# A hybrid decoder layer: convolution of the second tile back on VectorE, small ScalarE steps ahead of pair scalings, and a longer rotation of row slots

## The reference

```
proj = x @ w_in                      # q, k, v | index q, k, weights | z, xbc, dt
A    = sparse attention: 64 keys per query chosen by an index score, softmax, values
B    = Mamba-2 scan of silu(conv4(xbc)), two chunks of 128, gated RMS norm with silu(z)
h    = LayerNorm(alpha * x + concat(A, B) @ w_out)
for each of 8 heads:                 # PEER, "product keys"
    s1, s2 = halves of (h @ wq) against 128 keys each; top 16 of each
    best 16 of the 256 sums -> 16 expert numbers, gate = softmax(best)
    out += sum_k gelu(h . u[expert_k]) * gate_k * v[expert_k]
result = LayerNorm(alpha * h + out)
```

## Time and profile before

| what | value |
|---|---|
| median of 3 runs | 835.3 us (829.94 to 835.62) |
| profiled execution | 832.65 us, span 830.9 us, mean PE clock 0.83 |
| busy PE / DVE / ACT / POOL | 68% / 65% / 54% / 36% of the span |
| HBM read | 299.5 MB, mean 362 GB/s over the span |
| gathers | 256, 268.45 MB, 78.6% of 16 engines' span |
| first gather issued | 132.4 us |
| chain that ended last | DMA 40%, PE 26%, DVE 19%, ACT 6%, issue 6% |

### The profile page before, as it was taken

The page is one execution under the profiler, slowest core; times in us unless marked ns, Lnnn a source line. Parts: engine busy times, 40 slices in busy tenths (PEclk is TensorE's granted clock), DMA queues, the critical chain, the costliest instruction groups (busy, mean ns, idle before and its releaser), DMA issues.

```text
span 830.9 us, 10111 instructions
## 1 busy us (share of the span) xinstructions
PE 568.8 (68%) x3343; PEld 473.9 (57%) x3343; DVE 542.3 (65%) x1364; ACT 449.3 (54%) x805; POOL 297.9 (36%) x279
## 2 busy tenths in 40 slices
PE   7989999887879888864545555525566565454596
PEld 4458577575569887853544445524455564454542
DVE  3487574485777574848585858469857576767454
ACT  1025137455667665756565657527766566565532
POOL 0000005642444334453535353414754435344400
PEclk9989999899979899967878776767776767867789
DMA  8991005899999999999999999999999999999992
GB/s 300 386 355 52 1 1 204 297 397 354 341 416 411 410 410 410 419 421 422 422 420 422 420 420 420 422 421 382 411 421 421 421 423 422 422 421 423 422 422 109
DMA packets 58521, 301.08 MB, mean 362 GB/s; under 512 B 5576, under 2 KB 16112, under 8 KB 25712
## 3 DMA queue, kind: packets, MB, share of 16 engines
q0 software_dynamic: 36864, 268.45, 78.6%
q1 hardware_dynamic: 20400, 31.92, 10.8%
q10 hardware_dynamic: 1216, 0.19, 0.1%
HBM read 299.49 MB, written 1.05 MB: 362 GB/s over the span
## 4 chain that ended last, share of the span: by engine, by line
DMA 40%; PE 26%; DVE 19%; issue 6%; ACT 6%; POOL 2%; another core or an unknown queue 1%; DVEq 0%; SPq 0%; POOLq 0%; ACTq 0%
DMA arena<-in_expert_uv,expert 34%; PE bank L652 6%; PE bank L502 5%; DMA arena<-in_peer_wq 5%; PE bank L633 5%; DVE arena L1482 5%; PE bank L672 3%; ACT arena L1010 3%; PE bank L514 2%; POOL arena L455 1%; ACT weight L1000 1%; PE bank L617 1%; DVE score L1459 1%; DVE score L1461 1%
## 5 line engine op out<-in xcount | busy, mean ns | idle before, releaser
L455 POOL DMA_INDIRECT arena<-in_expert_uv,expert x256 | 281.4, 1099 | 489.5 <-PE bank L652 260.0
L652 PE MATMUL bank<-ident,arena 128*128 128x128 f32 x1920 | 302.7, 328 | 218.5 <-ACT arena L1010 211.8
L1482 DVE SCALAR_TENSOR_TENSOR arena<-x_sb,arena 128x1024 f32<-128x1024 f32 x256 | 307.9, 1229 | 172.0 <-DMA arena<-in_expert_uv,expert 168.5
L652 PEld LDWEIGHTS bank<-ident,arena 128*128 128x128 f32 x1920 | 279.9, 173 | 241.9 <-ACT arena L1010 233.2
L1010 ACT ACTIVATE arena<-arena,weight 128x1024 f32<-128x1024 f32 x240 | 257.1, 1138 | 2.2
L995 ACT ACTIVATE gelu<-dots 128x4 f32<-128x4 f32 (+2 forms) x76 | 15.5, 204 | 216.7 <-DVE arena L1482 209.1
L502 PE MATMUL bank<-arena,x_t 128*128 128x512 f32 (+1 forms) x128 | 55.1, 585 | 6.1 <-DMA arena<-in_w_idx 6.1
L633 PE MATMUL bank<-x_t,arena 128*128 128x128 f32 x384 | 50.9, 297 | 11.6 <-DMA arena<-in_peer_wq 11.6
L1000 ACT ACTIVATE weight<-gelu,gate 128x1 f32<-128x1 f32 x256 | 55.9, 284 | 3.5
L633 PEld LDWEIGHTS bank<-x_t,arena 128*128 128x128 f32 x384 | 49.7, 213 | 12.2 <-DMA arena<-in_peer_wq 12.2
L502 PEld LDWEIGHTS bank<-arena,x_t 128*128 128x128 f32 x128 | 25.3, 206 | 30.3 <-issue 26.4
(11 more groups left out here) (200 smaller groups left out, 487.6 us busy)
## 6 DMA issues: line engine op xcount, KB each, us to landing
arena<-in_w_in SPq DMA_DIRECT2D x5, 2048.0 KB, 19.8
arena<-in_peer_wq SPq DMA_DIRECT2D x6, 1024.0 KB, 7.4
arena<-in_w_out SPq DMA_DIRECT2D x2, 2048.0 KB, 18.2
arena<-in_expert_uv,expert POOLq DMA_INDIRECT x256
mix<-in_peer_wq SPq DMA_DIRECT2D x2, 1024.0 KB, 16.1
arena<-in_w_idx SPq DMA_DIRECT2D x4, 304.0 KB, 6.7
x_t<-in_x_columns SPq DMA_DIRECT2D x4, 256.0 KB, 5.8
x_sb<-in_w_in SPq DMA_DIRECT2D x1, 1024.0 KB, 9.5
```

Of the source, the lines that this page charges most:

```text
L455: pool.indirect_dma_start(out=arena[:, slot * SLOT:(slot + 1) * SLOT], out_offset=None, in_=expert_uv, in_offset=bass.IndirectOffsetOnAxis ...
L652: last = mm(banks[2 * tile + k // 4][:, (k % 4) * P:(k % 4 + 1) * P], lhsT=arena[:, at + k * P:at + (k + 1) * P], rhs=ident[:, :], is_tran ...
L1482: ins = stt(rows, x_rows[:, bass.ds(tile * D_MODEL, D_MODEL)], 1.0, rows, ALU.mult, ALU.mult, accum_out=dots[:, parity, j:j + 1])
```

## The change

- GpSimd's `convolve_late` and its tables go; VectorE runs `convolve(1, 0)` ahead of the first pair's dots and `convolve(1, 1)` behind them. Slot 1, where `xbc_raw` lies, waits for the convolution.
- `first_slots` has another order; slot 0 takes rows from the 15th gather on. For this, head 1's and 5's weights move into `big` (where q and k lay), loaded when tile 1's logits are done, and the transposed probabilities of tile 1 go into slot 0, over the logits, after all four transposes.
- Key scores of units 1 to 7 alternate between `mid` and `cb_masked`.
- ScalarE: scores, roots and gate exponentials move ahead of neighbouring pair scalings; TensorE's and VectorE's orders follow. `normalise` is split in two (`centre`, `spread`).
- VectorE rotates k's second tile after two of the eight selection rounds of tile 0.

```
-    start = [10, 11, 12, 13, 14, 15, 10, 11, 1, 5, 12, 13, 14, 15, 10, 11]
-    grow = [1, 5, 12, 13, 14, 15, 10, 11, 2, 1, 5, 12, 13, 8, 9, 14]
-    ring = [6, 7, 15, 10, 11, 2, 1, 5, 12, 13, 8, 9, 14]
-    return start + grow + 2 * ring + ring[:6] + ring[6:] + ring[:6] + [0, 4, 3]
+    start = [10, 11, 12, 13, 14, 15, 1, 10, 11, 12, 13, 5, 14, 15, 0, 1]
+    grow = [10, 11, 12, 13, 5, 14, 15, 0, 1, 10, 11, 2, 12, 8, 9, 13]
+    ring = [6, 7, 5, 14, 15, 0, 1, 10, 11, 2, 12, 8, 9, 13]
+    return start + grow + 2 * ring + ring[:4] + ring[4:] + ring[:4] + [4, 3]
...
-        probs_t = [view(mid, 2048, 1, HEADS, P), view(big, 0, TILES, HEADS, P)]
+        probs_t = [view(mid, 2048, 1, HEADS, P), view(arena, SCRATCH, TILES, HEADS, P)]
...
+            if h % 4 == 1:
+                return view(big, 0, KT, 2 * P)
...
-            wait_job(sp, ("T_p", 1, 3))
+            wait_job(sp, ("logits", 1, 3))
             load_head(1)
...
+                        elif slot == 1:
+                            pool.wait_ge(conv_ready, 2 * TILES)
...
-                    if isinstance(u, int) and u == 0 and j in LATE_TAPS:
-                        for n, k in LATE_TAPS[j]:
-                            convolve_late(n, k)
...
             queries(0, 1)
+            scores_of_keys(0, 1)
+            project(("proj_v", 1), "v", 1, ks=range(0, 4))
             sum_group(0, 1)
-            scores_of_keys(0, 1)
-            project(("proj_v", 1), "v", 1)
+            project(("proj_v", 1), "v", 1, ks=range(4, KT))
...
             y_diagonal(1)
+            queries(0, 2)
             sum_group(0, 4)
-            queries(0, 2)
-            sum_group(0, 5)
             scores_of_keys(0, 2)
             project_out(1, 0, ATTN)
-            sum_group(0, 6)
+            sum_group(0, 5)
             project_out(1, 1, ATTN)
             transposed_y(1)
+            sum_group(0, 6)
+            project_out(1, 0, SSD)
             sum_group(0, 7)
-            project_out(1, 0, SSD)
...
             weigh_slots(0, 0, 0)
-            weigh_slots(0, 0, 1)
-            take_queries(0, 1)
-            take_scores(0, 1)
             silu_z(1)
             silu_xbc(1, 0)
             silu_xbc(1, 1)
+            take_queries(0, 1)
+            take_scores(0, 1)
+            weigh_slots(0, 0, 1)
             weigh_slots(0, 0, 2)
             take_v(1)
+            exp_gate(act, 1)
             weigh_slots(0, 0, 3)
-            exp_gate(act, 1)
             take_mixed("T_attn", 0, attn_t_ready, 1)
             weigh_slots(0, 0, 4)
-            weigh_slots(0, 0, 5)
             take_queries(0, 2)
             root_of_squares(1)
+            take_scores(0, 2)
+            weigh_slots(0, 0, 5)
             weigh_slots(0, 0, 6)
-            take_scores(0, 2)
+            take_mixed("T_y", 4, y_t_ready, 1)
+            exp_gate(act, 2)
             weigh_slots(0, 0, 7)
-            take_mixed("T_y", 4, y_t_ready, 1)
             weigh_slots(1, 1, 0)
-            exp_gate(act, 2)
...
-            select_keys(0, range(TOPK_KEYS // 8))
+            select_keys(0, range(0, 2))
             rope_qk(1, 1)
+            select_keys(0, range(2, TOPK_KEYS // 8))
...
+            convolve(1, 0)
             dot_slots(0, 0, 0, 0)
+            convolve(1, 1)
             dot_slots(0, 0, 0, 1)
...
             dot_slots(0, 0, 0, 4)
-            finish_gate(1, 1)
             take_ssd(1)
             dot_slots(0, 0, 0, 5)
             scale_ssd(1)
-            dot_slots(0, 0, 0, 6)
+            finish_gate(1, 1)
             scores_in(0, 2)
             route_sides(2)
+            dot_slots(0, 0, 0, 6)
             dot_slots(0, 0, 0, 7)
```

More of the change, by code:

```diff
@@ L180, in build_layer @@
         attn = view(mid, 3072, HEADS, HEAD_DIM)
-        tap_product = view(arena, at + 1536, 4, P)
-        probs_t = [view(mid, 2048, 1, HEADS, P), view(big, 0, TILES, HEADS, P)]
+        probs_t = [view(mid, 2048, 1, HEADS, P), view(arena, SCRATCH, TILES, HEADS, P)]
         diag = view(mid, 1024, 8, P)
@@ L246, in build_layer @@
         z_ready, raw_ready, conv_ready, silu_ready, v_ready = (sem(n) for n in ("z_ready", "raw_ready", "conv_ready", "silu_ready", "v_ready"))
-        consts_t_ready, late_tap = sem("consts_t_ready"), sem("late_tap")
+        consts_t_ready = sem("consts_t_ready")
         decay_arg_ready, decay_ready, decay_masked = (sem(n) for n in ("decay_arg_ready", "decay_ready", "decay_masked"))
@@ L296, in head_weights @@
         def head_weights(h):
-            if h % 4:
-                return view(arena, (0, 4, 3)[h % 4 - 1] * SLOT, KT, 2 * P)
-            return view(mix, 1024, KT, 2 * P)
+            if h % 4 == 0:
+                return view(mix, 1024, KT, 2 * P)
+            if h % 4 == 1:
+                return view(big, 0, KT, 2 * P)
+            return view(arena, {2: 4, 3: 3}[h % 4] * SLOT, KT, 2 * P)
         def weight_rows(name, k, width=512):
@@ L319, in scores_at @@
         def scores_at(u):
-            if isinstance(u, int) and u < 2:
-                return view(mid, 2560, 2 * N_KEYS)
+            if isinstance(u, int) and u < PEER_HEADS:
+                return cb_masked[:, :, :].rearrange("p a b -> p (a b)") if u and u % 2 == 0 else view(mid, 2560, 2 * N_KEYS)
             return big[:, bass.ds(u * 2 * N_KEYS, 2 * N_KEYS)]
@@ L431, in _ @@
                       allow_small_or_imprecise_dtypes=True).then_inc(consts_ready, 1)
-            last_readers = {0: ("peer_q", 1, 5), 2: ("T_y", 1), 3: ("peer_q", 1, 7), 4: ("peer_q", 1, 6), 5: ("proj_v", 1),
+            last_readers = {0: ("pv", 1), 2: ("T_y", 1), 3: ("peer_q", 1, 7), 4: ("peer_q", 1, 6), 5: ("proj_v", 1),
                             6: ("out", 1, 1), 7: ("out", 1, 1), 8: ("out", 1, 0), 9: ("out", 1, 0), 10: ("proj_xbc", 1, 0),
@@ L448, in gather_unit @@
                             pool.wait_ge(slot_used, len(before) - before[::-1].index(slot))
-                        elif slot in last_readers:
+                        elif slot == 1:
+                            pool.wait_ge(conv_ready, 2 * TILES)
+                        else:
                             wait_job(pool, last_readers[slot])
@@ L926, in take_probs @@
             def take_probs(t):
+                wait_job(act, ("T_p", t, 2 * t + 1))
                 for n in range(2 * (t + 1)):
@@ L1364, in half_stats, with centre @@
                 link(nc.vector.bn_stats(stats[:, 6 * half:6 * half + 6], x_sb[:, t, part]))
-            def normalise(t, n, done):
+            halves = [slice(half * 512, (half + 1) * 512) for half in range(2)]
+            def centre(t):
                 link(nc.vector.bn_aggr(moments[:, :], stats[:, :]))
                 ts(rstd[:, :], moments[:, 1:2], LN_EPS, None, ALU.add).then_inc(var_ready, 1)
-                halves = [slice(half * 512, (half + 1) * 512) for half in range(2)]
                 for part in halves:
@@ L1373, in normalise, with spread @@
                 link(ins)
+            def spread(t, n, done):
                 dve.wait_ge(std_ready, n + 1)
@@ L1377, in normalise @@
                     stt(x_sb[:, t, part], x_sb[:, t, part], rstd[:, :], ln_gb[:, 1, part], ALU.mult, ALU.add).then_inc(done, 1)
+            def normalise(t, n, done):
+                centre(t)
+                spread(t, n, done)
             def add_mixed(t, half, part):
@@ L1522, in _ @@
             dot_slots(1, 0, 1, 0)
-            finish_gate(2, 0)
             dot_slots(1, 0, 1, 1)
@@ L1527, in _ @@
                 half_stats(1, half, add_mixed)
+            centre(1)
             dot_slots(1, 0, 1, 3)
-            normalise(1, 1, h_ready)
+            spread(1, 1, h_ready)
+            finish_gate(2, 0)
+            for g in range(4, 8):
+                dot_slots(1, 0, 1, g)
             dve.wait_ge(h_ready, 2 * TILES)
             dve.sem_inc(ln1_done, 1)
-            for g in range(4, 8):
-                dot_slots(1, 0, 1, g)
             for u in range(2, LOOP_FIRST):
```

2 lines of the change are left out of this document (1 added, 1 removed).

## The result

The changed kernel takes 828.0 us (median of 20 runs, 826.22 to 832.58) where the kernel before takes 834.4 us in as many runs; the ratio is 0.9945 with a 95% interval of 0.9925 to 0.9966. By this ratio the change gains 0.55%, about 4.6 us, beyond noise; the two medians are 6.4 us apart. Forecast were 15.9 us and 819 us, with 811 to 832 as the range: the time lies in the range, the gain is 29% of what was said by the ratio and 40% by the medians. The profiled execution took 826.22 us, span 824.5 us.

The account below looks back on a forecast made before the run. DMA gathers were taken as the bound, with 19.8 us of empty queue early on. Gains of 3.9 (rotation), 2.5 (second head's load) and 9.5 us (empty time) sum to 15.9 us, giving 819 us, range 811 to 832.

Parts of the forecast that it names:

- How the kernel is bound: Whole kernel: gathers fill the DMA engines from about 350 to 810 us; only empty time before about 260 us can change.
- the wait for the third head's weights: TensorE at the third head's queries: the sum counted no wait, with the queries ready at 169.4 us.
- rival C: TensorE stands for the third head's weights, landing at 199 us, holding sums and gathers: 10.7 us lost, 846 us; chance 0.07.
- signs of being wrong: GpSimd over 3 us at slot 1, TensorE standing at third head's queries, first gather at 132 us, or later stretches below 400 GB/s.
- Rotation: VectorE's rotation of k's second tile after two selection rounds ends TensorE's wait before its running sums: 3.9 us, first gather 128.5 us.
- Second head's weights early: Load issued near 110 us into idle engines instead of ahead of the first gather: 2.5 us of transfer leave the busy period.
- Taps to VectorE: Tile 1's late convolution leaves GpSimd, so nine gathers are asked for by 145.6 us, where the ninth was at 160.38.
- The wait at slot 1: Seventh gather waits for the convolution, asked for at 143.1 us; costs nothing unless the dots are over 2 us late.
- The price that the prediction worked out for the issues: Gather issues beside VectorE's taps may each grow at most 0.7 us; counted as nothing, 6.3 us if all nine were exposed.
- Small steps ahead of pair scalings: ScalarE's root before pair 5, with centring split from spreading: tile 1's layer norm moves from 235 to about 210 us, no gain.
- A: The chain of dots, scalings and sums stays the limit from 160 us on: gain 10.1 us, time 825 us; chance 0.20.
- B: Only the rotation counts, the queue's emptiness merely moves: gain 3.9 us, time 831 us; chance 0.13.

Follow-up runs that it names:

- e2: Changed kernel, but the third head's queries of the first tile use the second head's weights and skip their own wait: 818.0 us, ratio 0.9801.
- e1: Changed kernel with the fifth pair's sum put back ahead of the third head's queries in TensorE's order: 830.4 us, ratio 0.9954.
- e3: Kernel before the change with only the rotation moved between the selection rounds: 833.3 us, ratio 0.9977.
- e11: e9 with all eight selection rounds again ahead of the rotation: 821.4 us, ratio 0.9836.
- e10: e9 with the second head's weights again asked for right ahead of the first gather: 816.0 us, ratio 0.9772.
- e7: e4 with tile 1's convolution taps back on GpSimd instead of VectorE: 830.7 us, ratio 0.9967.
- e9: e8 plus the fill of e5, the best version: 815.6 us, ratio 0.9797 to the kernel before.
- e5: Changed kernel with two gate projection steps for tile 0 filling TensorE's 1.95 us pause before the scan's transposes: 826.75 us, ratio 0.9924.
- e12: e9 with two gate exponentials again behind the fourth and ninth pair's scalings: 816.15 us, ratio 0.9770.
- e8: Changed kernel with the third and seventh head's weights in slot 11, loaded ahead of the gathers, rows in slot 4: 821.4 us, ratio 0.9857.
- e4: Changed kernel where GpSimd waits for the third head's weights before its 13th gather: 822.9 us, ratio 0.9867.

## Why the prediction was wrong

- **How the kernel is bound: right.** From 340 to 800 us the engines move 420 GB/s (419 before), and only empty time before 260 us changed the end.
- **The step that failed is the wait for the third head's weights,** put at nothing in the sum and written off as rival C with 7 in 100. It measured 12.47 us of TensorE, and without it the kernel is 10.0 us faster (e2; 12 by the ratios). The order of queries and sum is not what failed: e1 has the old order and gains nothing. What failed is the load's landing, taken to be before 169.4 us. It came at 182, 24.0 us after it was asked for. That TensorE stands at these queries was one of the prediction's own signs of being wrong. Three readings led there. First, the median of 7.4 us over six loads was taken as the length in this stretch, where the trace before gives for these six:

```profile
DMA to landing us min/median/max: 5.6/7.4/57.4
```

The load asked for at 130.57 us took 5.6, the one at 202.42 took 7.4, and one into `mix` at 247.30 took 26.5. For the third head's, asked for at 165.39, that trace has no landing, since nobody waited for it; in the changed kernel, e1, e2 and e3 it took 24.0 to 27.3 us. Second, that the queries ran at 184.06 us without a wait was read as if the weights had long been there. The row shows only that they landed within 18.7 us. In e3, with the old order from 160 us on, TensorE waited 4.45 us for them: the kernel before was near the edge already, and the change moved the queries 14.5 us forward (184.06 to 169.55, when TensorE was ready) but the load only 7.4 (165.4 to 158.0). Third, the load was put beside two to four gathers; in the run there were eight.

- **C's own sizes:** it put the break-even at a load of 31.7 us and the loss at 42.25 us. A load of 24.0 us cost 10 to 12 us of the 15.9, near what its arithmetic (29.6 us less 3 for a landing at 199, hence 9.6 for 182) would have given. The mistake was in the chance and in taking the extreme row for the price; the middle of the range was left out. The load of 42.25 us had been asked for 5.3 us behind another head's, which itself took 26.5.
- **Rotation, 3.9 us: right in place, short on what comes next.** A pause of 1.95 us took the place of the 3.97, since the taps stood behind selection rounds, and after it the clock was at half in six profiles of seven. Alone it gave 1.9 us by the ratio (the interval reaches over 0, e3); with the new pause filled it is worth 5.4 us (e11 against e10), 3.97 us of waiting and the half clock behind it.
- **Second head's weights early, 2.5 us: not there, 0.4 us within noise (e10).** My sum counted the transfer as taken away and left 6.0 us of idle engines at 126 to 142 us standing, in which it fits. The same bytes cannot be a gain in a stretch that is already counted as empty.
- **Taps to VectorE: right, 7.8 us (e7, in a kernel that holds gathers back).** The wait at slot 1 did not show: GpSimd stood 0.30 to 0.31 us before each of the sixth to the ninth gather. In e9, with another order of slots, it stood 1.35 us there. The first dot takes 1.23 us without GpSimd's taps beside it (2.03). The Trainium skill (SBUF — State Buffer, "Who interferes with whom") has a VectorE instruction with two SBUF inputs contend with a GpSimd instruction that reads SBUF, and these two rows agree. The price that the prediction worked out for the issues did not appear: the issue beside VectorE's taps took 0.99 us (at 140.18), the next four 0.94 to 1.03. Other issues did take up to 2.0 us, for instance 2.01 and 1.99 beside two dots in e5.
- **Small steps ahead of pair scalings: right at nothing, as far as tested (e12, the two exponentials).**
- **A slip in the sum:** the first bytes are put 1.6 us behind the issue, but its own rows give 133.6 less 132.37, that is 1.2. It moves the sum by 0.4 us.
- **Rivals A and B: out.** With the wait gone, the chain of dots, scalings and sums lets the engines run at 405 to 418 GB/s from 160 to 235 us (e2, e12), and e2's 818.0 us is 7 under A's 825 and 13 under B's 831.

With the stall in place of the failed step the sum is 15.9 - 10 = 5.9 us, and 834.4 - 5.9 = 828.5 us against the measured 828.0. That it fits so well is in part luck, for errors on both sides offset each other: the 2.5 us of the early weights were not there, the rotation lost part of its gain to the new pause, and the taps' share was larger than the 3.7 us (9.7 less 6.0) that my sum gave the stretch to 160 us. How the rest divides was not measured. Why the fill gains 5.8 us in e9 and 1 to 2 in e5 stays open; the share of executions at half clock (five of six in e8, nine of 20 in the changed kernel, if the times are read so) would explain part of it.

## What to carry to other kernels

A wait that a trace does not show has a margin that it does not show either: before moving a consumer forward past other work, find when its data lands, not only that it was there, and move the load by as much. A median over loads that ran beside different things is no price for one of them. Here the third head's load took 11.6 to 27.3 us beside three or more gathers and 5.2 to 5.5 ahead of them; so issue it before the gathers start, or hold a few gathers back for it. And when a pause of TensorE goes, look for the next one at once, since a pause of 2 us could cost 3.3 us at half clock besides its own length.

## What the runs showed of the hardware

The same 1 MB load took 5.2 to 5.6 us when it was asked for ahead of the gathers (e8, e9, and the second head's in the kernel before), 11.6 beside three 1 MB gathers (e4), 24.0 beside eight and 25.8 beside ten. In the changed kernel the gathers beside it had nearly drained when it landed (the engines moved 386 GB/s at 175 to 180 us and 12 at 180 to 185, the landing being at 182). But that is not what ends it: where the gathers did not run dry, it landed after 26.0 us (e3, 416 GB/s from 178 to 186 us) and 27.3 us (e2, 411 GB/s from 160 to 235 us). The count alone does not give the length either: in the kernel before it took at most 18.7 us, though eight gathers were asked for in that time. The Trainium skill (DMA: Bandwidth & Descriptors, "Queues, rings and completion order") has each engine take turns between queues packet by packet. A load that is through after a fixed number of turns would land after much the same time whether eight gathers stand beside it or more, as it does here; no run varied the rows' size, so this stays an argument.

After TensorE had been busy without a break from 60 to 75.5 us and then stood 1.95 us, its granted clock was 0.50 to 0.62 from 78 to 84 us in six profiles and 1.00 in the changed kernel's, with the same instructions ahead of it; in the four with that pause filled (e5, e9, e10, e12) it was 1.00. After pauses of 8.67 us (e1), 12.47 us (the changed kernel) and 13.57 us (e5) it was at half each time.
